# Later divisions in the first mixers' attention, an early table load, a moved turn of y, and x turned in three pieces at a residual add

## The chip, the cores and the metric

The program runs on one core of one Trainium2 chip. The metric is the device time of one execution in microseconds (us). The engines are TensorE (PE in the rows, with its weight loads as PEld), VectorE (DVE), ScalarE (ACT), GpSimd (POOL) and SyncE (SP), which issues nearly all transfers. Each engine works through its own list of instructions in order and waits on semaphores that the others raise.

## The reference, cut to what matters

Twelve sublayers work on a state x of 256 rows by 1024 columns: feed-forward, mixer, feed-forward, four times over. The first two blocks use the mixer below (called the first mixers here), the last two another one, which the change leaves as it was.

```python
for l in range(DEPTH):                                   # DEPTH = 2
    h = rms_norm(x, ffn1_norm[l])
    x = x + FFN_RES_WEIGHT * swiglu(h, ffn1_wg[l], ffn1_wu[l], ffn1_wd[l])
    h = rms_norm(x, mix_norm[l])
    z = h @ w_in[l]
    rq, rk, rv, rg, mq, mk, mv, ca, cg = jnp.split(z, cuts, axis=-1)
    y_ret  = silu(rg) * normed(retention(rotary(rq), rotary(rk), rv))   # 6 heads of 64
    y_moba = moba_attention(rotary(mq), rotary(mk), mv)                 # 6 heads of 64
    y_conv = conv_module(ca, cg, conv_w[l], conv_b[l], conv_ln_g[l], conv_ln_b[l])  # 31 taps
    x = x + concatenate([y_ret, y_moba, y_conv]) @ w_out[l]
    h = rms_norm(x, ffn2_norm[l])
    x = x + FFN_RES_WEIGHT * swiglu(h, ffn2_wg[l], ffn2_wu[l], ffn2_wd[l])
```

With 256 rows there is one block of keys, so `moba_attention` is a causal softmax over 256 keys: scores, a mask, exp, a division by the row's sum, and the product with the values.

## The kernel before, in words

All products run at near full float32 accuracy: weight and activation are each split into a high part (`wh`, `xh`, by ACT) and a low part (`wl`, `xl`, by DVE), and TensorE adds three products: L1759 high by high, L1760 low weight by high, L1762 high weight by low. A weight arrives in one of four `raw` buffers, is split by ACT at L2076 into one of five `wh` slots and by DVE at L2357 into the `wl` slot of the same number. A "sub" is two blocks of 128 rows of a weight: 12 matmuls. In a mixer the high parts are made four subs ahead of the one that TensorE takes, the low parts three ahead.

The order is written out once, in class `Order`; every engine's class runs through the same calls and issues only its own share. So the place of a call in `Order` sets its place in the lists of all engines at the same time.

**Turning x.** Activations must stand with their columns on the partitions before TensorE can use them. `turn_x` transposes x on TensorE (L1732, 128 by 128, out of the identity in `cst`), `prep_hi` (ACT, L2103) and `prep_lo` (DVE, L2404) split the result, scaled by the norm's gain. x has two tiles of rows, t = 0 and 1, and two halves of columns, h = 0 and 1; a sublayer's last output GEMM ends with the sub-products of (t 0, h 1) and then (t 1, h 1), each followed by the addition to x on DVE (L2442 in feed-forwards, L2444 in mixers). The five sublayers that are followed by a plain norm end in `leave`. Before the change h = 0 is turned whole (8 transposes) during the second half's GEMM, and `leave` turns h = 1: four transposes of t = 0, then four of t = 1, which wait for the last addition.

**Attention of the first mixers.** Six heads go in three groups of two (`attention`). For each group: scores on TensorE (L1878); on DVE the mask, with the row's extreme (L2472); exp on ACT with the row's sum (L2150); then `normalize`: two reciprocals on DVE (L2482) and four divisions on ACT (L2166, the exp's rows times the reciprocal). Then come the transposes of the group's probabilities (`turn`: L1732 reading `pt`, three into bank 6 for the first head, three into bank 7 for the second), their copies to `ptT` by ACT (L2156), and the product with the values (`values`: L1904, always into bank 7), whose result ACT and DVE split into `y1h` (L2171) and `y1l` (L2497). Bank 7 is free again only when `y1l` is done, or, after transposed heads, when ACT has copied them (`Trq`, L2180).

Between these stand calls of `fill`, which take one sub each of the projection GEMMs (mv, rq, rk, rv, rg) and, when a chunk is complete, what belongs to it. For rq and rk that is `q_done`: three taps of the convolution on both column blocks (DVE, six instructions, L2536), two copies of the chunk's rows to `zt` (ACT, L2188), and the rotation (DVE, six instructions, L2511 to L2516). Its transposed heads are posted to a later `fill` (L1732 reading `zt`, into banks 6 and 7). In the first mixers the function handed in is `step_fill`: a `fill` and one more tap per `fill` (two instructions) if no chunk was completed. The second and third group have two subs before the values of the group before (`half` 0), and two behind them.

**After the attention** comes the retention, pair by pair (`ret_values`: L1959 to L1961, always into bank 7), mixed with the output GEMM's first subs. `turn_wo` turns normalized rows of `ym` (L1732 reading `ym`) into bank 6 or 7 in turn, and ACT (L2176) and DVE (L2502) split them. The bank is free when DVE is done. `turn_wo(0)` writes bank 7, in both versions.

Of the kernel before, what the change touches and what calls it, by code (L numbers as in the profile page):

```python
# [394 lines left out]
class Order:  # L395
# [248 lines left out]
        pass  # L644

    def prep(self, h, nx):
        p = self.prep_turn(h, (self.next_t(), self.next_t()))
        self.prep_hi(p, nx)
        self.prep_lo(p, nx)

    def prep_turn(self, h, bb):
        out = []
        for n in range(2):
            out.append((4 * h + 2 * n, bb[n], self.new(self.s.turned, "x")))
        self.turn_x(h, out)
        return out

    def turn_x(self, h, p):
        pass

    def prep_hi(self, p, nx):
# [16 lines left out]

    def enter(self, nx):

        for n, p in enumerate(self.prep_turn(0, (6, 7)) + self.prep_turn(1, (2, 3))):
            self.prep_hi([p], nx)
            self.prep_lo([p], nx)
            self.ahead(min(n + 1, 3), 0)
        for h in range(2):
            for t in range(2):
                self.square(t, h)
        self.row_scale()

    def leave(self, nx, bb):  # L690
        p = self.prep_turn(1, bb)
        self.prep_hi(p, nx)
        self.prep_lo(p, nx)
        self.square(1, 1)
        self.row_scale()

# [130 lines left out]
    def into_x(self, label, banks2, X, K, ready, ga, nx, hook, start=None, td=None):  # L827
        plain, turned, p = nx[0] == "plain", False, None
        for h in range(2):
            b, k = start[h] if start else (banks2(), 0)  # L830
            end = K if h == 0 else max(k, K - (4 if plain else 2 * TAIL))
            while k < end:
                n, td = self.gemm_sub(label, b, X, k, K, ready)
                k += n
                hook(h, k)
                if h == 1 and k == 4 and plain:
                    self.prep(0, nx)
                    turned = True
            if h == 0:
                b0 = b  # L840
                if isinstance(ga, tuple):
                    self.need_ada(ga[0], 6)
                if start and not plain:
                    self.ahead(5, 0)
                for t in range(2):
                    self.add_x(t, h, b[t], td, ga)
                for t in range(2):
                    self.square(t, 0)
        if not plain and nx[-1] is not None:
            self.need_ada(nx[-1], 4)  # L850
        self.split_sums()
        self.flush()
        two = [self.take(label) for _ in range((K - k) // 2)]
        self.ahead(3 if plain else 2, 0)
        first, last = (self.s.prod, ("tail", two[0][0])), (self.s.sub, two[-1][0])
        self.x_sum = last
        self.tail(0, two, b[0], X, k, K, ready)
        if plain and not turned:
            p = self.prep_turn(0, (self.next_t(), self.next_t()))
        self.add_x(0, 1, b[0], first, ga)  # L860
        if p:
            self.prep_hi(p, nx)
        self.square(0, 1)
        self.tail(1, two, b[1], X, k, K, ready)
        if plain:
            self.add_x(1, 1, b[1], last, ga)
            if p:
                self.prep_lo(p, nx)
            self.leave(nx, b0)
            return  # L870
        self.normed(0, nx)

        def add_1(between=lambda: None):
            self.add_x(1, 1, b[1], last, ga, between)
        if nx[-1] is not None:
            self.half = nx, add_1
            return
        add_1()
        self.square(1, 1)
        self.normed(1, nx)  # L880
# [93 lines left out]
    def attention(self, groups, fill, last):  # L974

        n = len(groups)
        for g in range(n + 1):
            if g:
                self.turn(groups[g - 1])
            if g < n:  # L980
                self.scores(groups[g])
            else:
                last(0)
            ahead = [st for st in groups[g + 1] if st.pre is not None] if g + 1 < n else []
            for st in ahead:
                st.pre[0](st)
            subs = 1 if g == 0 else len(groups[min(g, n - 1)])
            for half in range(2 if g < n else 1):
                if half == 1 and len(ahead) == 2:
                    ahead[1].pre[1](ahead[1])  # L990
                for i in range(subs):
                    fill()
                    if i == 0 and half == 0:
                        if ahead:
                            ahead[0].pre[1](ahead[0])
                        if g < n:
                            self.normalize(groups[g])
                    if g == n:
                        last(i + 1)
                if g and half == 0 and groups[g - 1].pairs:  # L1000
                    self.values(groups[g - 1])
# [176 lines left out]
    def mix1(self, l, nx):  # L1178
# [57 lines left out]
            self.fill()  # L1236
            taps(1)

        def step_fill():
            n = len(self.jobs)  # L1240
            self.fill()
            taps(1 if len(self.jobs) == n else 0)

        steps = []
# [56 lines left out]
        def turn_wo(i):  # L1301
            tiles = (WO_TILES[1][1:],) + WO_TILES[2:]
            after = [[yret.get(0)], [normed], [yret.get(1), yret.get(2)]][i]
            pos = (3, 4, 6)[i]
            done = self.turn_y(tiles[i], after, pos, "y1")
            for n in range(len(tiles[i])):
                ytok[pos + n] = done
# [30 lines left out]
        ret_norm(0)  # L1338
        step()
        self.ret_sum(l, 1)  # L1340
        turn_wo(0)
        step()
        ret_out(2)
        ret_norm(1)
        step()
# [50 lines left out]
    def mix2(self, l, a, nx):  # L1396
# [197 lines left out]
            if i < 2:  # L1594
                gates(0, i)

        self.attention(groups, self.fill, last_values)
        while len(self.jobs) > 1 or self.jobs[0]["k"] < 6:
            self.fill()
        last_b = self.jobs[0]["b"]  # L1600
# [124 lines left out]
class Tensor(Order):  # L1725
# [59 lines left out]
        e.matmul(m.ps[b], m.onesr[:, :], m.ach[:, :], start=True, stop=False)  # L1785
        self.then_inc(e.matmul(m.ps[b], m.onesr[:, :], m.acl[:, :], start=False, stop=True), (s.prod, ("red", q)))

    def turn_x(self, h, p):
        m = self.m
        for t in range(2):  # L1790
            for k, b, tk in p:
                self.wait_ge(self.xr[t, h], self.free[b])
                for kk in range(2):
                    ins = self.transpose(m.ps[b][:, kk * 256 + t * P:kk * 256 + (t + 1) * P],
                                         m.x[:, t, (k + kk) * P:(k + kk + 1) * P])
                if t:
                    self.then_inc(ins, tk)
# [250 lines left out]
class Scalar(Order):  # L2048
# [144 lines left out]
    def glu(self, b, tk, u):  # L2193
        m = self.m
        for t in range(2):
            self.wait_ge(tk, self.rr_at, self.zt_free[0])
            self.then_inc(self.e.activation(m.zt[0][:, t, 0:256], m.ps[b[t]][:, 256:512], ACT.Sigmoid,
                                            scale=m.rr[:, t:t + 1]), (self.s.act, ("sigmoid", u[t][1])))

    def turn_u(self, b, after, tk, tp):  # L2200
        m = self.m
# [720 lines left out]
```

## Time and profile before

| | us |
|---|---|
| median of three runs | 2228.94 |
| lowest, highest | 2228.0, 2229.93 |
| the profiled execution, its own time | 2229.7 |
| its span in the trace | 2227.9 |
| PE busy, of the span | 2196.3 (99%) |
| DVE busy | 1536.2 (69%) |
| ACT busy | 1153.5 (52%) |
| POOL busy | 53.3 (2%) |

All times of rows are us from the span's start. The stages that the change touches are the first mixers, which lie at about 202 to 319 and 696 to 815, and the five ends of sublayers at 201, 318, 505, 695 and 814. A matmul is modelled as pipelined: a row's start against the next row's start is its share of time, its duration is longer. "x6" is six like instructions in one row. A bracket behind a row tells how long the engine stood idle before it and what ended that. Idle time of TensorE is time of the program unless it is made up later; idle time of the others costs nothing as such.

### The profile page before, as it was taken

What the parts mean: (1) busy time and instruction counts of PE and PEld (TensorE: products, weight loads), DVE (VectorE), ACT (ScalarE), POOL (GpSimd) and SP (SyncE); (2) the same over time, 40 slices, a digit from 0 to 9 for tenths busy, and PEclk for the clock granted to TensorE, in tenths of its full rate; (3) what the DMA queues carried; (4) which work ended last, traced back from release to release, by engine and by line L of the source; (5) the groups of instructions that cost most, each with busy time, mean ns of one, the idle gap of its engine ahead of it and who ended that gap; (6) DMA issues with size and microseconds to landing.
All of it is one profiled execution on the core that took longest, in us unless ns stands there. A gap on an engine that the chain in (4) does not pass through costs nothing.

```text
span 2227.9 us, 27041 instructions
## 1 busy us (share of the span) xinstructions
PE 2196.3 (99%) x10840; PEld 1842.4 (83%) x10840; DVE 1536.2 (69%) x2342; ACT 1153.5 (52%) x1782; POOL 53.3 (2%) x46
## 2 busy tenths in 40 slices
PE   8999999999999999999999999999999999999998
PEld 7888888888888888887888987888888889778887
DVE  5655975557886978867886655878678856557664
ACT  5445654444445654445445666544454456556443
POOL 0000010000000010001001000100000010001000
PEclk9999999999999999999999999999999999999999
DMA  8554454556875457775876444578768864445653
GB/s 287 191 194 155 150 177 171 188 195 232 284 280 161 150 192 264 264 263 180 282 277 193 157 133 148 187 269 284 265 215 283 286 192 140 144 151 171 235 198 123
DMA packets 250641, 462.92 MB, mean 208 GB/s; under 512 B 9798, under 2 KB 55792, under 8 KB 250388
## 3 DMA queue, kind: packets, MB, share of 16 engines
q1 hardware_dynamic: 250276, 461.04, 61.5%
q8 instruction: 85, 1.39, 0.2%
q14 instruction: 40, 0.33, 0.0%
q10 hardware_dynamic: 240, 0.16, 0.0%
HBM read 460.12 MB, written 1.05 MB: 207 GB/s over the span
## 4 chain that ended last, share of the span: by engine, by line
PE 91%; DVE 6%; ACT 2%; issue 0%; DMA 0%; POOL 0%; ACTq 0%; DVEq 0%; POOLq 0%
PE ps L1759 18%; PE ps L1762 18%; PE ps L1760 18%; PE s L1759 8%; PE s L1762 8%; PE s L1760 8%; PE ps L1732 4%; DVE wl L2357 1%; PE s L1878 1%; PE ps L1775 1%; PE ps L1773 1%; PE ps L1774 1%; PE ps L1904 1%; PE ps L1805 1%; DVE gts L2712 1%; PE ps L1838 1%
## 5 line engine op out<-in xcount | busy, mean ns | idle before, releaser
L2357 DVE TENSOR_TENSOR wl<-raw,wh 128x1024 fp32r<-128x1024 f32 (+2 forms) x732 | 851.1, 1180 | 219.0 <-ACT wh L2076 213.6
L2076 ACT ACTIVATE wh<-raw 128x1024 fp32r<-128x1024 f32 (+2 forms) x744 | 750.4, 1026 | 471.0 <-PE ps L1762 266.7
L1759 PE MATMUL ps<-wh,xh 128*128 128x512 f32 (+3 forms) x1632 | 621.5, 381 | 1.0 <-DVE wl L2357 1.0
L1762 PE MATMUL ps<-wh,xl 128*128 128x512 f32 (+3 forms) x1632 | 610.6, 374 | 0.0
L1760 PE MATMUL ps<-wl,xh 128*128 128x512 f32 (+3 forms) x1632 | 610.4, 374 | 0.0
L1759 PEld LDWEIGHTS ps<-wh,xh 128*128 128x128 f32 x1632 | 307.4, 188 | 55.7 <-issue 9.0
L1762 PEld LDWEIGHTS ps<-wh,xl 128*128 128x128 f32 x1632 | 307.2, 188 | 47.4
L1760 PEld LDWEIGHTS ps<-wl,xh 128*128 128x128 f32 x1632 | 307.7, 189 | 44.7
L2365 DVE SCALAR_TENSOR_TENSOR acc<-raw,condT,acc 128x512 f32<-128x512 f32 x252 | 188.7, 749 | 5.1
L1759 PE MATMUL s<-wh,xh 128*128 128x512 f32 x384 | 150.3, 391 | 0.0
L1762 PE MATMUL s<-wh,xl 128*128 128x512 f32 x384 | 149.6, 390 | 0.0
L1760 PE MATMUL s<-wl,xh 128*128 128x512 f32 x384 | 149.5, 389 | 0.0
L1759 PE MATMUL s<-wh,hTh 128*128 128x512 f32 x352 | 138.5, 393 | 0.0
L1762 PE MATMUL s<-wh,hTl 128*128 128x512 f32 x352 | 137.3, 390 | 0.0
L1760 PE MATMUL s<-wl,hTh 128*128 128x512 f32 x352 | 137.1, 390 | 0.0
L2143 ACT ACTIVATE hTh<-ps 128x512 fp32r<-128x512 f32 x88 | 48.3, 596 | 162.7 <-PE ps L1732 162.7
L2464 DVE TENSOR_TENSOR hTl<-ps,hTh 128x512 fp32r<-128x512 f32 x88 | 57.0, 686 | 104.3 <-ACT hTh L2143 104.3
L1759 PE MATMUL ps<-wh,hTh 128*128 128x512 f32 x268 | 104.5, 390 | 0.0
L1762 PE MATMUL ps<-wh,hTl 128*128 128x512 f32 x268 | 104.3, 389 | 0.0
L1760 PE MATMUL ps<-wl,hTh 128*128 128x512 f32 x268 | 104.3, 389 | 0.0
L1762 PEld LDWEIGHTS s<-wh,xl 128*128 128x128 f32 x384 | 72.1, 188 | 15.1
L1759 PEld LDWEIGHTS s<-wh,xh 128*128 128x128 f32 x384 | 72.1, 188 | 14.8
(348 smaller groups left out, 2495.0 us busy)
## 6 DMA issues: line engine op xcount, KB each, us to landing
raw<-in_ffn_w_in SPq DMA_DIRECT2D x80, 1024.0 KB, 5.3
raw<-in_ada_w SPq DMA_DIRECT2D x72, 1024.0 KB, 5.6
raw<-in_ffn_wg SPq DMA_DIRECT2D x40, 1024.0 KB, 5.3
raw<-in_ffn_wu SPq DMA_DIRECT2D x40, 1024.0 KB, 5.3
raw<-in_ffn_wd SPq DMA_DIRECT2D x40, 1024.0 KB, 5.2
raw<-in_ffn_w_out SPq DMA_DIRECT2D x40, 1024.0 KB, 5.7
raw<-in_mix_w_in SPq DMA_DIRECT2D x28, 1024.0 KB, 5.2
raw<-in_w_in SPq DMA_DIRECT2D x28, 768.0 KB, 4.5
```

What stands on the lines that cost most here:

```text
L1732: return self.e.transpose(out, src, self.m.ident[0:n, 0:n])
L1759: e.matmul(o, X[0](kk, t), hi, start=kk == 0, stop=False)
L1760: e.matmul(o, X[0](kk, t), lo, start=False, stop=False)
L1762: ins = e.matmul(o, X[1](kk, t), hi, start=False, stop=kk == K - 1)
L1773: e.matmul(o, X[0](kk, t), hi, start=kk == 0, stop=False)
L1774: e.matmul(o, X[0](kk, t), lo, start=False, stop=False)
L1775: ins = e.matmul(o, X[1](kk, t), hi, start=False, stop=kk == K - 1)
L2076: ins = self.e.activation(m.wh[j % NH][:, 0:n], m.raw[u % NR][:, k0 * w:k0 * w + n], ACT.Copy)
L2143: self.then_inc(self.e.activation(m.hTh[:, k:k + 2, :].rearrange("p k s -> p (k s)"), m.ps[b], ACT.Copy), th)
L2357: ins = self.e.tensor_tensor(m.wl[j % NH][:, 0:n], m.raw[u % NR][:, k0 * w:k0 * w + n], hi, ALU.subtract)
L2365: ins = self.e.scalar_tensor_tensor(out=a, in0=m.raw[u % NR][:, k * 512:k * 512 + 512], scalar=m.condT[:, kk:kk + 1], in1=a if kk else m.b ...
L2464: self.then_inc(self.e.tensor_tensor(lo, m.ps[b], hi.bitcast(F32), ALU.subtract), tl)
```

## The change

It does four things. First, in the first mixers `normalize` of a group is called inside the step: for the first group behind the `fill` but ahead of the step's tap; for the second and third group not in the first of the two steps but in the second one (`i == subs - 1`), behind everything that `fill` issues there. In the second mixers the order is as before. Second, behind the sigmoid of the convolution's gate ACT gets a one-element exp, so that the exp table is loaded there and not at the first softmax. Third, a `step` (one sub) that stood behind `turn_wo(0)` now stands ahead of it. Fourth, h = 0 of x is turned early in its first bank alone (4 transposes and not 8); `leave` turns (t 0, h 1), then the other bank of h = 0 (4 transposes, both tiles), then (t 1, h 1), and splits the three banks behind that.

```diff
--- before.py
+++ after.py
@@ -644,18 +644,20 @@
         pass
 
     def prep(self, h, nx):
-        p = self.prep_turn(h, (self.next_t(), self.next_t()))
+        p = self.prep_turn(h, {0: self.next_t()})
         self.prep_hi(p, nx)
         self.prep_lo(p, nx)
 
+    def prep_new(self, h, bb):
+
+        return [(4 * h + 2 * n, bb[n], self.new(self.s.turned, "x")) for n in bb]
+
     def prep_turn(self, h, bb):
-        out = []
-        for n in range(2):
-            out.append((4 * h + 2 * n, bb[n], self.new(self.s.turned, "x")))
-        self.turn_x(h, out)
-        return out
-
-    def turn_x(self, h, p):
+        p = self.prep_new(h, bb)
+        self.turn_x(h, p, range(2))
+        return p
+
+    def turn_x(self, h, p, rows):
         pass
 
     def prep_hi(self, p, nx):
@@ -678,7 +680,7 @@
 
     def enter(self, nx):
 
-        for n, p in enumerate(self.prep_turn(0, (6, 7)) + self.prep_turn(1, (2, 3))):
+        for n, p in enumerate(self.prep_turn(0, {0: 6, 1: 7}) + self.prep_turn(1, {0: 2, 1: 3})):
             self.prep_hi([p], nx)
             self.prep_lo([p], nx)
             self.ahead(min(n + 1, 3), 0)
@@ -688,9 +690,13 @@
         self.row_scale()
 
     def leave(self, nx, bb):
-        p = self.prep_turn(1, bb)
-        self.prep_hi(p, nx)
-        self.prep_lo(p, nx)
+
+        p0, p1 = self.prep_new(0, {1: self.next_t()}), self.prep_new(1, dict(enumerate(bb)))
+        self.turn_x(1, p1, (0,))
+        self.turn_x(0, p0, range(2))
+        self.turn_x(1, p1, (1,))
+        self.prep_hi(p0 + p1, nx)
+        self.prep_lo(p0 + p1, nx)
         self.square(1, 1)
         self.row_scale()
 
@@ -856,7 +862,7 @@
         self.x_sum = last
         self.tail(0, two, b[0], X, k, K, ready)
         if plain and not turned:
-            p = self.prep_turn(0, (self.next_t(), self.next_t()))
+            p = self.prep_turn(0, {0: self.next_t()})
         self.add_x(0, 1, b[0], first, ga)
         if p:
             self.prep_hi(p, nx)
@@ -989,12 +995,16 @@
                 if half == 1 and len(ahead) == 2:
                     ahead[1].pre[1](ahead[1])
                 for i in range(subs):
-                    fill()
-                    if i == 0 and half == 0:
-                        if ahead:
+
+                    norm = half == 0 and g < n and i == (subs - 1 if groups[g][0].by_act else 0)
+                    matrix = half == 0 and i == 0 and ahead
+
+                    def behind():
+                        if matrix:
                             ahead[0].pre[1](ahead[0])
-                        if g < n:
+                        if norm:
                             self.normalize(groups[g])
+                    fill(behind)
                     if g == n:
                         last(i + 1)
                 if g and half == 0 and groups[g - 1].pairs:
@@ -1236,9 +1246,10 @@
             self.fill()
             taps(1)
 
-        def step_fill():
+        def step_fill(norm):
             n = len(self.jobs)
             self.fill()
+            norm()
             taps(1 if len(self.jobs) == n else 0)
 
         steps = []
@@ -1338,8 +1349,8 @@
         ret_norm(0)
         step()
         self.ret_sum(l, 1)
+        step()
         turn_wo(0)
-        step()
         ret_out(2)
         ret_norm(1)
         step()
@@ -1594,7 +1605,11 @@
             if i < 2:
                 gates(0, i)
 
-        self.attention(groups, self.fill, last_values)
+        def fill(norm):
+            self.fill()
+            norm()
+
+        self.attention(groups, fill, last_values)
         while len(self.jobs) > 1 or self.jobs[0]["k"] < 6:
             self.fill()
         last_b = self.jobs[0]["b"]
@@ -1785,9 +1800,9 @@
         e.matmul(m.ps[b], m.onesr[:, :], m.ach[:, :], start=True, stop=False)
         self.then_inc(e.matmul(m.ps[b], m.onesr[:, :], m.acl[:, :], start=False, stop=True), (s.prod, ("red", q)))
 
-    def turn_x(self, h, p):
-        m = self.m
-        for t in range(2):
+    def turn_x(self, h, p, rows):
+        m = self.m
+        for t in rows:
             for k, b, tk in p:
                 self.wait_ge(self.xr[t, h], self.free[b])
                 for kk in range(2):
@@ -2196,6 +2211,8 @@
             self.wait_ge(tk, self.rr_at, self.zt_free[0])
             self.then_inc(self.e.activation(m.zt[0][:, t, 0:256], m.ps[b[t]][:, 256:512], ACT.Sigmoid,
                                             scale=m.rr[:, t:t + 1]), (self.s.act, ("sigmoid", u[t][1])))
+
+        self.e.activation(m.small[:, 240:241], m.phalf[:, 0:1], ACT.Exp)
 
     def turn_u(self, b, after, tk, tp):
         m = self.m
```

What stands in a row on the engines, at the three places that matter. Line numbers of the changed kernel are 15 to 17 higher for the same operation.

DVE, second group of a first mixer. Before; `RECIPROCAL` belongs to the second group's division, the six rows with `rt` and `zt` are the rotation of rq:

```order
L2357 TENSOR_TENSOR wl_64<-raw_53,wh_59 128x768
L2536 SCALAR_TENSOR_TENSOR cacc<-upad,cols_68,cacc 128x256 x2
L2482 RECIPROCAL small<-small 128x2 x2
L2357 TENSOR_TENSOR wl_65<-raw_54,wh_60 128x768
L2536 SCALAR_TENSOR_TENSOR cacc<-upad,cols_68,cacc 128x256 x6
L2511 TENSOR_TENSOR rt_131<-zt_104,cos_72 128x384
L2512 TENSOR_TENSOR rt_132<-zt_104,sin_73 128x384
L2513 TENSOR_TENSOR rt_133<-zt_104,cos_72 128x384
L2514 TENSOR_TENSOR rt_134<-zt_104,sin_73 128x384
L2515 TENSOR_TENSOR zt_104<-rt_131,rt_132 128x2x6x32
L2516 TENSOR_TENSOR zt_104<-rt_133,rt_134 128x2x6x32
L2497 TENSOR_TENSOR y1l<-ps,y1h 128x256
```

DVE at the same place in the changed kernel:

```order
L2553 SCALAR_TENSOR_TENSOR cacc<-upad,cols_68,cacc 128x256 x2
L2374 TENSOR_TENSOR wl_65<-raw_54,wh_60 128x768
L2553 SCALAR_TENSOR_TENSOR cacc<-upad,cols_68,cacc 128x256 x6
L2528 TENSOR_TENSOR rt_131<-zt_104,cos_72 128x384
L2529 TENSOR_TENSOR rt_132<-zt_104,sin_73 128x384
L2530 TENSOR_TENSOR rt_133<-zt_104,cos_72 128x384
L2531 TENSOR_TENSOR rt_134<-zt_104,sin_73 128x384
L2532 TENSOR_TENSOR zt_104<-rt_131,rt_132 128x2x6x32
L2533 TENSOR_TENSOR zt_104<-rt_133,rt_134 128x2x6x32
L2499 RECIPROCAL small<-small 128x2 x2
L2514 TENSOR_TENSOR y1l<-ps,y1h 128x256
```

The two reciprocals moved behind a `wl`, six tap instructions and the rotation, and stand directly ahead of `y1l`. The third group is the same, with rk.

ACT, second group. Before; `pt_107` and `pt_108` are the two heads' probabilities, divided in four instructions:

```order
L2076 ACTIVATE wh_60<-raw_54 128x768
L2166 ACTIVATE pt_107<-pt_107,small 128x128
L2166 ACTIVATE pt_107<-pt_107,small 128x256
L2166 ACTIVATE pt_108<-pt_108,small 128x128
L2166 ACTIVATE pt_108<-pt_108,small 128x256
L2076 ACTIVATE wh_61<-raw_54 128x768
L2188 ACTIVATE zt_104<-ps,rr 128x384 x2
L2171 ACTIVATE y1h<-ps 128x256
L2076 ACTIVATE wh_57<-raw_55 128x768
```

ACT at the same place in the changed kernel:

```order
L2091 ACTIVATE wh_60<-raw_54 128x768
L2091 ACTIVATE wh_61<-raw_54 128x768
L2203 ACTIVATE zt_104<-ps,rr 128x384 x2
L2181 ACTIVATE pt_107<-pt_107,small 128x128
L2181 ACTIVATE pt_107<-pt_107,small 128x256
L2181 ACTIVATE pt_108<-pt_108,small 128x128
L2181 ACTIVATE pt_108<-pt_108,small 128x256
L2186 ACTIVATE y1h<-ps 128x256
L2091 ACTIVATE wh_57<-raw_55 128x768
```

The divisions moved behind a `wh` and the two `zt`, and stand directly ahead of `y1h`. In the third group the transposed heads' copies `Trq` stand between the two `wh`, so the divisions moved behind them too.

PE around `turn_wo(0)`. Before (the two transposes of `ym`, then a whole sub of 12 matmuls, of which the first three rows are shown, then the retention's products, not shown):

```order
L1762 MATMUL ps<-wh_60,y1l 128x512
L1732 MATMUL ps<-cst,ym 128x128 x2
L1759 MATMUL ps<-wh_61,y1h 128x512
L1760 MATMUL ps<-wl_66,y1h 128x512
L1762 MATMUL ps<-wh_61,y1l 128x512
```

PE in the changed kernel:

```order
L1774 MATMUL ps<-wh_61,y1h 128x512
L1775 MATMUL ps<-wl_66,y1h 128x512
L1777 MATMUL ps<-wh_61,y1l 128x512
L1747 MATMUL ps<-cst,ym 128x128 x2
L1974 MATMUL ps<-rv,pt_107 128x64
L1975 MATMUL ps<-rv,pt_107 128x64
L1976 MATMUL ps<-rv,pt_107 128x64
```

The transposes of `ym` moved behind that sub, and the retention's products, which write the same bank 7, follow them directly.

## Rows read from the trace of the kernel before

**Rows 1.** What TensorE waited for in the whole program: us, times, longest:

```profile
PE ps L1904 <- ACT Trq L2180: 3.8, 2, 1.9
...
PE s L1732 <- DVE x L2442: 1.0, 3, 0.3
```

**Rows 2.** Timeline (start, duration, instruction), PE, a sublayer's end:

```profile
200.35 0.60 PE L1732 MATMUL s<-cst,x 128*128 128x128 f32 x4
201.30 0.66 PE L1732 MATMUL s<-cst,x 128*128 128x128 f32 x4 [0.35 <-DVE x L2442]
```

**Rows 3.** The same place, DVE:

```profile
200.55 0.69 DVE L2442 SCALAR_TENSOR_TENSOR x<-ps,x 128x512 f32<-128x512 f32 x1 [2.03 <-PE ps L1775]
```

**Rows 4.** Timeline, PE, attention of the first mixer without its subs:

```profile
256.74 0.91 PE L1732 MATMUL ps<-cst,pt 128*128 128x128 f32 x6
257.58 0.93 PE L1878 MATMUL s<-Tmk,Tmq 64*128 64x128 f32 x8
...
265.47 0.87 PE L1904 MATMUL ps<-ptT,mv 128*64 128x256 f32 x8 [1.92 <-ACT Trq L2180]
270.56 0.82 PE L1732 MATMUL ps<-cst,pt 128*128 128x128 f32 x6
271.13 0.42 PE L1759 MATMUL ps<-wh,xh 128*128 128x384 f32 x1
```

**Rows 5.** Timeline, DVE, first group's masks, then second and third group:

```profile
241.72 0.08 DVE L2472 DVE_READ_ACCUMULATOR2_ANT small<- 128x1 f32 x1
...
253.63 0.55 DVE L2511 TENSOR_TENSOR rt<-zt,cos 128x384 f32<-128x384 f32 x1
...
256.57 0.42 DVE L2497 TENSOR_TENSOR y1l<-ps,y1h 128x256 fp32r<-128x256 f32 x1
...
262.99 0.22 DVE L2482 RECIPROCAL small<-small 128x2 f32<-128x2 f32 x2
263.18 0.96 DVE L2357 TENSOR_TENSOR wl<-raw,wh 128x768 fp32r<-128x768 f32 x1
264.06 2.46 DVE L2536 SCALAR_TENSOR_TENSOR cacc<-upad,cols,cacc 128x256 f32<-128x256 f32 x6
```

**Rows 6.** Timeline, ACT, table load and the groups:

```profile
240.73 1.28 ACT L2150 ACT_TABLE_LOAD   x1
242.03 0.41 ACT L2150 ACTIVATE pt<-pt,small 128x128 f32<-128x128 f32 x1
...
260.54 0.40 ACT L2150 ACTIVATE pt<-pt,small 128x128 f32<-128x128 f32 x1 [2.37 <-DVE small L2472]
...
262.31 0.83 ACT L2076 ACTIVATE wh<-raw 128x768 fp32r<-128x768 f32 x1
263.18 1.49 ACT L2166 ACTIVATE pt<-pt,small 128x128 f32<-128x128 f32 x4
264.57 0.84 ACT L2180 ACTIVATE Trq<-ps 128x512 f32<-128x512 f32 x2
```

**Rows 7.** Timeline, PE, turn of ym:

```profile
294.59 0.44 PE L1732 MATMUL ps<-cst,ym 128*128 128x128 f32 x2 [0.24 <-DVE ym L2600]
...
297.62 0.33 PE L1959 MATMUL ps<-rv,pt 128*128 128x64 f32 x2
```

**Rows 8.** The same place, ACT:

```profile
295.06 0.38 ACT L2176 ACTIVATE y1h<-ps 128x256 fp32r<-128x256 f32 x1 [0.50 <-PE ps L1732]
```

**Rows 9.** Second mixer, PE, same places as rows 4:

```profile
759.58 1.42 PE L1904 MATMUL ps<-ptT,mv 128*64 128x256 f32 x8 [1.92 <-ACT Trq L2180]
...
766.25 0.81 PE L1732 MATMUL ps<-cst,pt 128*128 128x128 f32 x6
```

**Rows 10.** Stretches: us; busy (count) of PE, PEld, DVE, ACT, POOL; clock; DMA:

```profile
194.00:330.00 136.00, 132.90 (x751) 117.54 (x750) 107.73 (x225) 82.54 (x155) 6.91 (x6) 1.00 0.49 155
...
260.00:270.00 10.00, 8.08 (x52) 7.41 (x51) 9.36 (x27) 8.38 (x21) 0.00 (x0) 1.00 0.53 171
...
755.00:765.00 10.00, 8.08 (x43) 7.09 (x42) 9.35 (x24) 7.83 (x21) 0.00 (x0) 0.83 0.41 136
```

## Prediction

> **What bounds the kernel now.** I read the busy times first: TensorE is busy 99% of the span, so only what adds to or takes from its list or its idle time counts. Then the waits of TensorE [rows 1]: those at this change are two waits of 1.9 us for `Trq`, one in each first mixer, and short ones for the last addition to x, three of 0.35 in feed-forwards shown and two like them in mixers. Then the timelines around them, engine by engine. The reader is to see in [rows 4] that TensorE has its last sub before `values` behind it at 265.47 - 1.92 = 263.55, and in [rows 6] why it waits: ACT does the four divisions (263.18) ahead of the `Trq` copies (264.57), and these free bank 7. In [rows 5] DVE's y1l starts at 256.57, directly behind the rotation, and TensorE's `turn` starts at 256.74 [rows 4] and needs that y1l for its second bank: DVE sets that point with nearly no slack.
>
> **Part 1, x turned in three pieces: a gain.** The number of transposes stays 16 at each of five places; four move from an earlier point, where TensorE is never idle, into the wait. Four cost (201.30 - 200.35) less the wait. The first four start at 200.35, the next at 201.30, a distance of 0.95 [rows 2]; DVE's addition ends at 200.55 + 0.69 = 201.24 [rows 3]. At 0.11 each (0.57 over six in [rows 4], 270.56 to 271.13, gives 0.095) four take 0.38 to 0.44, so the distance holds eight of them and 0.1 is left. Gain 0.43 each, 2.15 over five. Behind it ACT splits three banks in a row and not two; the first product needs only the bank that was turned early, and the next one comes a sub later, so I count nothing. Bounds: 0.35 (the idle time shown) and 0.51 (the whole wait) each, 1.75 to 2.55.
>
> **Part 2, the table load.** It takes 1.28 and ends at 242.03, where the first exp starts [rows 6]. Without it exp starts when DVE has read out the row's extreme, at 241.72 + 0.08 = 241.80 [rows 5], and a signal, 241.85: 0.18 earlier. Everything that hangs on ACT there comes that much earlier. Bounds 0 and 0.23. In its new place it costs ACT 1.28 and an exp of at most 0.41. ACT is busy 82.5 of 136 us in this stretch [rows 10] and its `wh` run four subs ahead, which hides it; without that cover it would be 1.7 a mixer.
>
> **Part 3, the divisions of the second and third group: a loss.** The aim shows in the third group: `Trq` comes before the divisions. But `normalize` as a whole moved, reciprocals included, and DVE reaches them only behind six taps and the rotation. ACT blocks at the divisions until then, and queued behind them on ACT is `y1h`; behind that, on DVE, `y1l`; behind that, on TensorE, the second bank of `turn`. A chain that ran beside the rotation now runs after it.
>
> Second group, on the clock of the trace. The rotation ends at 256.57 [rows 5], less the 0.18 of part 2: 256.39. Reciprocal and its signal 0.2 (0.19 from 262.99 to 263.18): 256.6. Four divisions 1.4 (263.18 to 264.57 [rows 6]): 258.0. `y1h` 0.38 (size of [rows 8]) and signal: 258.41. `y1l` 0.42 [rows 5] and signal: 258.9, where before it was 257.05. So the second three transposes, and the scores behind them, are 1.85 late.
>
> Third group. DVE's list from y1l to the masks is the same and without idle time, so the exps, released at 260.54 before [rows 6], come at 262.4 and end 1.77 later, at 264.15. One `wh` (0.75 to 0.87) and now at once the `Trq` copies: 264.95. TensorE could start `values` 0.9 later (264.57 to 265.47): 265.85, against 265.47. The second group's loss eats the gain, and 0.4 is lost. DVE meanwhile: the second `wl` waits for its `wh`, 265.0; `wl` 0.88 and six taps 2.38 [rows 5] end at 268.3; the rotation takes 256.57 - 253.63 = 2.94, to 271.2 (its rows, two copies of `zt`, are there at 267.5). Then the same chain: reciprocal 271.4, divisions to 272.8, y1h to 273.2, y1l to 273.65, second bank of the turn at 273.7, three transposes 0.33: 274.0. Before, the sub there starts at 271.13 [rows 4]. Loss 2.9 in each first mixer, 5.8 together, as the two mixers' rows agree (265.47 and 759.58 with the same 1.92). Behind it nothing is owed: all weights' splits are at least a sub early, and retention starts when TensorE does. Bounds: 1.2 each, if the second bank waited for the divisions alone and not for y1l (y1h and y1l, 0.85 with signals, out of the chain in both groups), and 3.6, if the early table gives nothing and each of the chain's five links takes 0.1 more.
>
> **Part 4, `turn_wo(0)` a sub later: a small loss.** The wait that it is to remove is 0.4 (0.24 as idle time, the distance from the last matmul 0.4 more than usual) [rows 7]. But the transposes now write bank 7 directly ahead of the retention's products, which write bank 7 too. Without the wait the sub would start at 294.19 and end at 296.9; two transposes; ACT's y1h starts 0.47 behind their start (294.59 to 295.06, [rows 7, 8]), at 297.4, takes 0.38; y1l 0.42; signals 0.1: 298.3. Before, the products started at 297.62 [rows 7]. Loss 0.65 each, 1.3 together. Bounds: 0 (the split overlaps something that I don't see) and 1.9 a mixer (a `wl` of 1.2 ahead of y1l on DVE still running).
>
> **Sum.** 5.8 + 1.3 - 2.15 = +4.95. On the profiled execution (span 2227.9, its own time 2229.7) that is 2234.6; it lies 0.76 above the median of the runs, and the range of the runs, 1.9, is as wide as the clock item below. I set it on the median: 2228.94 + 4.95 = 2233.9.
>
> **The clock.** In the second mixer the 1.92 us wait is followed by a stretch at the lower level: the granted clock is 0.83 over 755 to 765, against 1.00 over 260 to 270 behind the same wait in the first [rows 10]. From `values` to `turn` it takes 766.25 - 759.58 = 6.67 [rows 9] against 270.56 - 265.47 = 5.09 [rows 4]: a fall to 1.2 GHz costs 1.58 here and follows one of two like waits. The changed kernel has no single wait of 1.92, but two near each other in the third group (about 0.9 and 1.4 with two or three transposes between) and two smaller in the second. A fall in the second group would be covered by the third group's wait. I count as many falls as before, one, and keep zero and two.
>
> The Trainium skill, in "TensorE: Matmul & The Clock Gate", section "Why this matters for your kernels", warns only of idle gaps that are clearly longer than all those here. By that rule the changed kernel would have no fall at all. The trace disagrees for a gap of 1.92, after which the clock did fall once.
>
> **Rivals.**
> A, no fall of the clock: no single new wait is as long as 1.92. The 1.58 goes: +3.4, 2232.3. For it: the waits are split. Against: together they are longer than before. Chance 0.25.
> B, falls in both first mixers: +6.5, 2235.5. For it: the pair of waits is 2.3 in 2.8 us. Chance 0.25.
> C, on the other side, faster: the divisions' new place doesn't decide, because DVE has done the rotation long before TensorE is at the `turn`. It would need the rotation to end 2.2 us earlier, before 254.4. Then `Trq` is copied at 263.2, `values` starts at 264.1, 1.4 earlier, and with the table 0.18: -3.2 for both, -2.15 for x, +1.3 for part 4, and with the clock -1.6: 2223.3 to 2224.9. Against: taps and rotation stand without a gap up to 256.57. Chance 0.07.
> D, the chains overlap more than I see, by the lower bounds of parts 3 and 4: 2.4 + 0 - 2.15: +0.25, 2229.2. Chance 0.08.
> My forecast as it stands: 0.35.
>
> **Range and chances.** 0.2% is 4.5 us, about what a measurement can tell from no change, and my sum lies just above it. Faster is C: 0.07. Within 0.2%: A and D whole, and a part of the forecast's own spread of about 1 us: 0.35. Slower: 0.58. The range goes from D's side, 2230.3, to above B, 2237.5; what is left out is C, most of D and the upper bounds.
>
> **What would show it.** Right: in the trace after, TensorE waits at `turn` for `y1l` in the second and third group, about 1.5 us each; ACT idle ahead of the divisions, released by the reciprocal; `values` waits well under 1 us; the retention's third products wait about 1 us for a y1l; no wait of 0.35 at the five additions. Wrong: if `turn` starts without a wait in the third group, part 3 falls and with it the sign; if x's five places still wait, part 1; if the falls of the clock are of another number, the time is off by 1.6 for each.

## The result, and the profile after

| | before | after |
|---|---|---|
| median, us (13 runs each) | 2228.52 | 2234.96 |
| lowest, highest | 2226.69, 2230.17 | 2232.63, 2236.64 |
| the profiled execution, its own time | 2229.7 | 2233.15 |
| its span | 2227.9 | 2231.3 |

The ratio is 1.0029, with a 95% interval of 1.0022 to 1.0037: 4.9 to 8.2 us slower. The forecast was 2233.9 in a range of 2230.3 to 2237.5, the forecast sum +4.95.

The waits of TensorE in the changed kernel (us in total, times, longest) show the signs that were named; only the waits for `y1l` at the turns, named as about 1.5 each, are 1.07. The two waits of 1.9 for `Trq` [rows 1] and the five for the addition to x are gone; new are four waits for `y1l` at the turns, and two at the retention's products. Of the waits for `Trq` one of 0.4 is left, in the first mixer:

```profile
PE ps L1747 <- DVE y1l L2514: 4.3, 4, 1.1
...
PE ps L1974 <- DVE y1l L2519: 1.9, 2, 0.9
...
PE ps L1747 <- ACT pt L2181: 1.4, 3, 0.8
...
PE ps L1919 <- ACT Trq L2195: 0.4, 1, 0.4
```

To lay one timeline on the other a common point is needed. The first transposes of `hb`, long before the change, stand here before:

```profile
46.62 1.03 PE L1732 MATMUL ps<-cst,hb 128*128 128x128 f32 x8
```

and here after:

```profile
44.67 1.03 PE L1747 MATMUL ps<-cst,hb 128*128 128x128 f32 x8
```

This execution was 1.95 us ahead before the change had touched anything: the loads at the program's start vary. The x turn at 200 adds 0.46, so 2.41 is added to a row of after in the first mixer to put it on the clock of the rows before.

TensorE after, second and third group of the first mixer, without the subs:

```profile
254.62 0.84 PE L1747 MATMUL ps<-cst,pt 128*128 128x128 f32 x3 [0.31 <-ACT pt L2181]
256.52 0.52 PE L1747 MATMUL ps<-cst,pt 128*128 128x128 f32 x3 [1.07 <-DVE y1l L2514]
256.97 0.93 PE L1893 MATMUL s<-Tmk,Tmq 64*128 64x128 f32 x8
...
263.34 0.87 PE L1919 MATMUL ps<-ptT,mv 128*64 128x256 f32 x8 [0.42 <-ACT Trq L2195]
...
269.41 0.83 PE L1747 MATMUL ps<-cst,pt 128*128 128x128 f32 x3 [0.81 <-ACT pt L2181]
271.32 0.52 PE L1747 MATMUL ps<-cst,pt 128*128 128x128 f32 x3 [1.07 <-DVE y1l L2514]
```

What was one row of six transposes [rows 4] is now two rows of three, each behind a wait. The scores stood at 257.58, now at 256.97 + 2.41 = 259.38: 1.80 late. `values` stood at 265.47, now at 265.75: 0.28 late, although its wait shrank from 1.92 to 0.42. DVE after, the same two groups:

```profile
253.50 0.55 DVE L2533 TENSOR_TENSOR zt<-rt,rt 128x384 f32<-128x384 f32 x1
253.97 0.22 DVE L2499 RECIPROCAL small<-small 128x2 f32<-128x2 f32 x2
255.95 0.42 DVE L2514 TENSOR_TENSOR y1l<-ps,y1h 128x256 fp32r<-128x256 f32 x1 [1.76 <-ACT y1h L2186]
...
268.76 0.22 DVE L2499 RECIPROCAL small<-small 128x2 f32<-128x2 f32 x2
270.75 0.43 DVE L2514 TENSOR_TENSOR y1l<-ps,y1h 128x256 fp32r<-128x256 f32 x1 [1.76 <-ACT y1h L2186]
```

and ACT after:

```profile
254.16 1.49 ACT L2181 ACTIVATE pt<-pt,small 128x128 f32<-128x128 f32 x4 [3.93 <-DVE small L2499]
255.56 0.36 ACT L2186 ACTIVATE y1h<-ps 128x256 fp32r<-128x256 f32 x1
...
268.96 1.49 ACT L2181 ACTIVATE pt<-pt,small 128x128 f32<-128x128 f32 x4 [3.99 <-DVE small L2499]
```

Read the three together. ACT stands idle for 3.93 us, released by the reciprocal, which DVE starts only as the rotation ends. Then DVE is idle for 1.76, released by `y1h`, and TensorE for 1.07, released by `y1l`. The idle times pass from engine to engine, which is the mark of a chain made serial.

### The profile page after: what moved, and what is told of

Same layout as the page of the kernel before. It is cut to its first block, busy times and chain, and to the rows that moved or that the text cites. A ratio compares the mean times of both kernels' runs of the same rounds, so it can differ in the third digit from the quotient of the medians.

```text
span 2231.3 us, 27045 instructions
## 1 busy us (share of the span) xinstructions
PE 2197.6 (98%) x10840; PEld 1842.8 (83%) x10840; DVE 1537.0 (69%) x2342; ACT 1153.7 (52%) x1784; POOL 55.2 (2%) x46
## 4 chain that ended last, share of the span: by engine, by line
PE 90%; DVE 7%; ACT 2%; DMA 0%; issue 0%; POOL 0%; ACTq 0%; DVEq 0%; POOLq 0%; SPq 0%
PE ps L1774 18%; PE ps L1777 18%; PE ps L1775 18%; PE s L1777 8%; PE s L1774 7%; PE s L1775 7%; PE ps L1747 3%; DVE wl L2374 2%; DVE cacc L2553 1%; PE s L1893 1%; PE ps L1790 1%; PE ps L1788 1%; PE ps L1789 1%; PE ps L1919 1%; PE ps L1820 1%; DVE gts L2729 1%
## 5 line engine op out<-in xcount | busy, mean ns | idle before, releaser
L2111 ACT ACTIVATE junk<-x 128x512 f32<-128x512 f32 x56 | 35.6, 636 | 95.0 <-DVE x L2461 59.1
```

Of the source, the lines that this page charges most:

```text
L2111: self.then_inc(self.e.activation(m.junk[:, :], m.x[:, t, h * 512:(h + 1) * 512], ACT.Square, scale=1.0 / 32, accum_out=m.ssq[:, 2 * h + t ...
```

## The experiments

Those with an interval were run side by side with the kernel before, whose median was 2228.8 beside x, turn_wo, the attention's part and the first of the two faster kernels, 2229.09 beside the single groups, the early reciprocals alone and the last of the faster kernels, and 2228.7 beside the table. "Faster" and "slower" in us are that median times the distance of the ratio from 1; the plain difference of the medians can differ from it by up to 0.8. "Landmark" means the start of a given row of TensorE, compared between two traces.

**One part alone: x.** Only the fourth edit of the change (`prep_turn` with one bank, `leave` with three pieces).

> The kernel before with x turned in three pieces at the five residual adds, and nothing else. Theory (the losses lie in the attention and at turn_wo(0), x is a gain): 2.2 us faster than before, 0.43 at each of the five places, and no wait of 0.35 left there. Rival (three banks split in a row cost what the filled wait gives): no change, and in the trace a new wait at the first products behind the turns.

Measured: 2226.61, ratio 0.9988 (0.9979 to 0.9996), 2.2 faster. The landmarks behind the five places come 0.43 to 0.46 earlier each, and all five waits are gone. Part 1 stands, with its size.

**One part alone: turn_wo(0).**

```diff
-        turn_wo(0)
         step()
+        turn_wo(0)
```

> The kernel before with turn_wo(0) moved behind the step, and nothing else. Theory: 1.3 us slower than before; the retention's third products wait about 0.95 us in each first mixer for y1l, which frees bank 7, and the wait of 0.4 at the transposes is gone. Rival (the move does what it seems to be for): 0.8 us faster, 0.4 at each of two places.

Measured: 2228.47, ratio 0.9998 (0.9989 to 1.0006). The time can't tell: 0.8 faster and 1.3 slower both lie within this interval. Nor can the two spans, as this profile lacks a fall of the clock in the second mixer that costs 1.6 in the one of before. TensorE's list can. The first retention products after the turn (297.62 before, [rows 7]):

```profile
297.95 0.43 PE L1959 MATMUL ps<-rv,pt 128*128 128x64 f32 x2 [0.93 <-DVE y1l L2502]
```

This trace runs 0.28 ahead at the third group's product with the values (276.99 before), so the row is 0.33 + 0.28 = 0.61 late, and as much in the second mixer. The wait of 0.24 for `ym` became one of 0.93 for `y1l`.

**One part alone: attention.** The new place of `normalize`, with x, table and turn_wo as before.

```diff
+    norm = half == 0 and g < n and i == (subs - 1 if groups[g][0].by_act else 0)
...
-                        if g < n:
+                        if norm:
                             self.normalize(groups[g])
```

> The kernel before with normalize called inside the step (reciprocals and divisions late in the second and third group), and nothing else. Theory: 6 us slower than before, less up to 1.6 where a fall of the clock behind the old wait of 1.9 us is gone; TensorE waits at turn for y1l in both groups. Rival (the loss comes from the early table load or the moved turn): no change or faster by up to 2.8, the two waits for Trq.

Measured: 2235.7, ratio 1.003 (1.002 to 1.004), 6.7 slower. The landmarks of the first mixer move by +3.06, those of the second by the same once the fall of the clock that before had there is taken out (+3.07 against the second profile of before, told below, which has none there). That is 6.1 for both mixers, beside 1.2 lost at turn_wo(0) and 2.2 gained at x: this part makes nearly all of the loss.

**Which group?** The same, for one group alone; for the third, `g == 2`:

```diff
-    norm = half == 0 and g < n and i == (subs - 1 if groups[g][0].by_act else 0)
+    norm = half == 0 and g < n and i == (1 if g == 1 and groups[g][0].by_act else 0)
```

> Only the second group's reciprocals and divisions go behind the last sub (the third group's stay in their old place; x, table and turn_wo as before). Theory (the chain reciprocal, divisions, y1h, y1l behind the rotation): the second three transposes of the turn at 257 us and the scores start 2.0 us late (1.85 and the 0.18 that the early table does not give here), the exps and the third group's divisions and Trq copies with them; `values` still waits about 1.9 for Trq, nothing is given back: +2.0 in each first mixer, 4.1 together, less up to 1.6 if the fall of the clock does not come. No wait for y1l at the third group's turn. Rival 1 (the loss arises in the third group alone; in the second, slack on ACT takes it up): the landmarks of TensorE at `values` move by less than 0.5, the time by less than 1. Rival 2 (the whole 3.1 of a mixer arises in the second group): +6.

> Only the third group's reciprocals and divisions go behind its last sub. Theory: the Trq copies come directly behind a wh, `values` starts 1.4 to 1.5 earlier in each first mixer and waits about 0.4; the rotation ends at about 269.4, reciprocals, four divisions, y1h and y1l follow, the second three transposes of the turn can start at 271.9 and the sub at 272.2, where it was 271.13: +1.1 a mixer, 2.2 together, within 1.6 for the clock. With the kernel of the second group alone this adds up to the 3.1 a mixer of both groups. Rival (the second group is innocent, all 3.1 come from the third): +6. Rival 2 (the aim is reached once the second group is left alone): the turn does not wait, 1.4 faster a mixer.

Measured: second group 2231.91, ratio 1.0015 (1.0006 to 1.0024), 3.3 slower; third group 2232.0, ratio 1.0011 (1.0002 to 1.002), 2.4 slower; together 5.7, beside 6.7 for both at once, within the intervals. (By the plain medians the two are 2.8 and 2.9, so the times don't rank them; the traces do.) TensorE with the second group alone late:

```profile
259.47 0.52 PE L1740 MATMUL ps<-cst,pt 128*128 128x128 f32 x3 [1.07 <-DVE y1l L2505]
259.91 0.93 PE L1886 MATMUL s<-Tmk,Tmq 64*128 64x128 f32 x8
...
267.67 0.87 PE L1912 MATMUL ps<-ptT,mv 128*64 128x256 f32 x8 [1.80 <-ACT Trq L2188]
```

and with the third alone late:

```profile
264.02 0.87 PE L1912 MATMUL ps<-ptT,mv 128*64 128x256 f32 x8 [0.39 <-ACT Trq L2188]
...
270.09 0.83 PE L1740 MATMUL ps<-cst,pt 128*128 128x128 f32 x3 [0.83 <-ACT pt L2174]
272.00 0.52 PE L1740 MATMUL ps<-cst,pt 128*128 128x128 f32 x3 [1.07 <-DVE y1l L2505]
```

The first of them is 0.35 behind before the attention begins. The scores are 1.98 late and `values` is 1.85 late, still behind a wait of 1.80 where it was 1.92: only 0.13 is given back. In the second, `values` comes 1.41 early, and the stretch from there through the turn with its two waits is 2.59 longer, +1.18 in all. Each group has its own loss, so both rivals that gave it one place fall, and 1.85 + 1.18 = 3.03 is the 3.06 of both. The second group's loss is what keeps the early `Trq` from paying.

**The reciprocals or the divisions?** Here the reciprocals go out in the step's first sub, ahead of its tap, and the divisions alone go behind the last sub.

```diff
                     def behind():
                         if matrix:
                             ahead[0].pre[1](ahead[0])
+                        if half == 0 and i == 0 and g < n:
+                            self.invert(groups[g])      # DVE: the reciprocals alone
                         if norm:
                             self.normalize(groups[g])   # ACT: the divisions alone
```

> Reciprocals go out in the step's first sub, ahead of the tap; the divisions behind the last one; x, table and turn_wo as before. Theory: no turn waits for the divisions; `values` starts 1.5 earlier in each first mixer, of which 0.7 to 0.75 is given back at the third group's turn, where y1l stands behind the rotation: 1.5 faster together, 3.1 if the fall of the clock after `values` goes as well. Rival (it was the divisions' place itself that cost, not the reciprocals'): 2 to 6 slower, the turns wait about 1 for y1l in both groups.

> The changed kernel with turn_wo(0) back in its old place, and with normalize in two parts: the reciprocals in the first step, ahead of the tap, in all three groups; the divisions on ACT in the last step. Theory (what costs is that the reciprocals moved behind the rotation on DVE, not that the divisions moved on ACT): turn no longer waits for y1l in the second and third group, Trq is copied 1.4 us earlier, values waits 0.5 and not 1.9: 2.2 for x, 0.4 for the table, 2.8 for the two waits, up to 1.6 for a fall of the clock: 5.4 to 7 us faster than before, about 2222. Rival (the divisions' place on ACT, behind two more wh and zt, delays y1h and with it bank 7 whatever DVE does): turn still waits over 1 us in each group, and the kernel is at most 1 us faster than before.

Measured: alone 2227.16, ratio 0.9991 (0.9982 to 0.9999), 2.0 faster; with x in three pieces and the early table (the changed kernel but for the reciprocals and turn_wo) 2224.65, ratio 0.998 (0.9971 to 0.9989), 4.5 faster. So the late place of the divisions costs nothing that shows; what made the loss is that DVE reached the reciprocals behind a `wl`, six taps and a rotation. The sum that I expected for the second, 5.4 to 7, was too good: it counted 2.8 for the two waits, and what follows shows that only about half of that was kept. TensorE in it, third group's turn:

```profile
266.82 0.49 PE L1756 MATMUL ps<-cst,pt 128*128 128x128 f32 x3
267.84 0.52 PE L1756 MATMUL ps<-cst,pt 128*128 128x128 f32 x3 [0.54 <-ACT ptT L2180]
```

DVE at the same place:

```profile
266.81 0.55 DVE L2545 TENSOR_TENSOR zt<-rt,rt 128x384 f32<-128x384 f32 x1
267.28 0.42 DVE L2526 TENSOR_TENSOR y1l<-ps,y1h 128x256 fp32r<-128x256 f32 x1
```

From the first group's scores on, TensorE now comes 1.6 earlier to the turn, 0.2 of it from the table, and 0.73 is given back there. The row names ACT's `ptT`, but `y1l`, done at 267.70, is a candidate too.

**Which of the two?** One tap of three is moved from ahead of the last rotation to a sub behind the turn, in the kernel just told.

```diff
             def done(b, tk):
-                taps(3)
+                taps(2 if n == "rk" else 3)
...
         def first_pair(i):
+            if i == 1:
+                taps(1)
```

> As the kernel with split reciprocals, x in three pieces and the early table, and one tap of three (two instructions of 0.41) moved from ahead of the last rotation to a sub behind the turn. What the trace of that kernel leaves open is what its third group's turn waits for (0.54, put down to ACT's ptT; DVE's y1l ends 0.13 earlier). Theory 1 (y1l, which stands behind taps and rotation on DVE): y1l ends 0.8 earlier, the wait of about 0.6 at the second three transposes goes, 0.6 to 0.75 gained in each first mixer: 5.5 to 6 faster than the kernel before. Theory 2 (ACT's ptT behind two wh): the wait stays at 0.5 and the time at 4.5 faster than before.

Measured, in five runs: 2222.45, ratio 0.9967 (0.9955 to 0.998), 7.4 faster than before (4.5 to 10.0), the lowest median of all. Its interval overlaps that of the kernel just told; the traces tell the two apart: from the first group's scores to the third group's product with the values it takes 0.73 less in the first mixer and 0.77 less in the second. The turn is one row of six again:

```profile
266.89 0.82 PE L1758 MATMUL ps<-cst,pt 128*128 128x128 f32 x6
```

because on DVE

```profile
266.58 0.42 DVE L2528 TENSOR_TENSOR y1l<-ps,y1h 128x256 fp32r<-128x256 f32 x1
```

ends, at 267.00, before the second bank is wanted, while ACT starts `ptT` no earlier than in the other kernel (267.42, 267.34 there). So it was `y1l`, and the releaser in brackets was the wrong one; there `y1l` and `ptT` had ended 0.13 apart.

**The table alone.**

```diff
+        self.e.activation(m.small[:, 240:241], m.phalf[:, 0:1], ACT.Exp)
```

> Only the exp table is loaded early. Theory: the first exp of the first mixers starts 0.18 earlier and all behind it as far as the wait for Trq, where the same 0.18 stays gained: 0.36 faster together, not to be told from no change by the time; `values` starts at 265.3 from the same start, with the same wait of 1.9. Rival (the load in its new place delays a wh or the exps of another group): 0.5 to 3 slower.

Measured: 2229.0, ratio 1.0 (0.9991 to 1.0009). The first exp is 0.19 earlier, as forecast, but TensorE's turn of that group gains only 0.04 and `values` 0.02 (265.47 to 263.68, in a trace that is 1.77 ahead). DVE with the table alone:

```profile
242.51 0.23 DVE L2484 RECIPROCAL small<-small 128x2 f32<-128x2 f32 x2
```

and ACT:

```profile
242.71 1.50 ACT L2166 ACTIVATE pt<-pt,small 128x128 f32<-128x128 f32 x4
```

The first group's divisions wait for a reciprocal that stands behind a tap. In the changed kernel the reciprocal is ahead of that tap, at 241.09:

```profile
241.09 0.41 DVE L2499 RECIPROCAL small<-small 128x2 f32<-128x2 f32 x2
```

and there the first group's turn does gain 0.19. With the attention's part alone it gains 0.00. At this turn neither edit is worth more than 0.04 without the other.

**The same two kernels once more.** Both were profiled a second time, unchanged, for the clock.

> The kernel before, word for word, profiled once more. If the falls of the clock belong to a kernel's order of work, the granted clock is 0.83 over 755 to 765 and 1.00 over 1000 to 1010 as in the first trace. If they differ from execution to execution, the fall behind the wait for Trq at 759.6 may be absent (the times then 1.6 shorter from there on), while every wait and distance in TensorE's list is the same within 0.1.

> The changed kernel, word for word, profiled once more. By order of work: falls again at 754 (granted clock 0.83 over 750 to 760) and two between 1000 and 1020 (0.83 over 1000 to 1010, 0.84 over 1010 to 1020). By execution: at least one of the three is elsewhere or absent; the waits for y1l at the turns stay at four of about 1.07.

The second profile of before, stretches of the first and the second mixer behind their waits for `Trq` (columns as in rows 10):

```profile
260.00:270.00 10.00, 8.07 (x44) 7.03 (x43) 9.36 (x28) 7.60 (x20) 0.00 (x0) 0.83 0.60 180
...
755.00:765.00 10.00, 8.08 (x52) 7.41 (x52) 9.39 (x27) 7.52 (x20) 0.00 (x0) 1.00 0.60 185
```

In the first profile it was the other way round [rows 10]. So the place of the fall belongs to the execution and not to the kernel's list. After, first and then second profile:

```profile
750.00:760.00 10.00, 8.55 (x45) 7.18 (x45) 8.13 (x23) 7.67 (x21) 0.00 (x0) 0.83 0.35 107
```

```profile
765.00:775.00 10.00, 8.03 (x40) 7.21 (x39) 8.20 (x18) 5.14 (x11) 0.00 (x0) 0.83 0.30 91
```

Up to 814 these two second profiles have one fall each that costs time, so they can be laid over each other as the forecast did. Before, from the first transposes of `hb` to the last addition's first transposes in the second mixer:

```profile
47.23 1.03 PE L1732 MATMUL ps<-cst,hb 128*128 128x128 f32 x8
...
813.55 0.60 PE L1732 MATMUL ps<-cst,x 128*128 128x128 f32 x4
```

and after:

```profile
46.90 1.03 PE L1747 MATMUL ps<-cst,hb 128*128 128x128 f32 x8
...
818.11 1.60 PE L1747 MATMUL ps<-cst,x 128*128 128x128 f32 x12
```

766.32 and 771.21: 4.89 longer, where the sum said 4.95. All five gains at x lie in it: the fifth is four transposes that left their place ahead of the last row.

## Why the prediction was right

**Part 1.** Forecast 0.43 at each of five places, measured 0.43 to 0.46. The alone kernel is 2.2 faster, forecast 2.15.

**Part 2.** The first exp came 0.18 to 0.19 earlier, and in the changed kernel the turn of the first group too. That the table alone would bring it was my working, and that was wrong: the step "everything that hangs on ACT there comes that much earlier" left out that the divisions also hang on the reciprocal, behind a tap. It came out right by luck, because part 3 moves that reciprocal. For the sum, which took both, this changed nothing.

**Part 3.** The chain came out link by link. On the clock of before: reciprocal done at 253.97 + 0.22 + 2.41 = 256.60 (forecast 256.6), y1h started at 257.97 (divisions done, 258.0), second half of the turn at 258.93 (258.9), scores 1.80 late (1.85). `values` at 265.75 (265.85). Third group: second half of the turn at 271.32 + 2.41 = 273.73 (273.7). All of it 2.88 a mixer, forecast 2.9; the attention's part alone, without the early table, 3.06. The aim was reached, `Trq` did come early, and two things ate it, as forecast: the second group's loss and the third group's own chain. DVE also stands idle for 1.76 in each chain, with `wl` and taps queued behind `y1l`, which the text did not price. Nothing of it showed on TensorE.

The waits at the turns were named as about 1.5 each. They are two waits, 0.31 and 1.07 in the second group, 0.81 and 1.07 in the third: the first three transposes wait for the divisions already, which the text did not say.

**Part 4.** Forecast 0.65, measured 0.61 a mixer alone and 0.63 in the changed kernel (the wait for `y1l` is 0.93, the one that went 0.24).

**The sum.** +4.95 forecast, 4.89 by the traces with equal falls up to 814, +6.4 by the medians with an interval of 4.9 to 8.2, so the sum lies at the interval's lower end. (The median of before fell by 0.42 with ten more runs, so the forecast time itself is 1.1 below the measured one.) Behind 814 there is more, which I did not forecast. At the next blocks' conditioning sums TensorE waits for `acl`, in the first profile of after:

```profile
936.00 0.50 PE L1800 MATMUL ps<-ach,onesr 128*128 128x512 f32 x1 [0.26 <-DVE acl L2389]
```

which costs 0.43 there, 0.52 in the second profile, 0.42 with the attention's part alone, 0.19 with x alone and 0.82 in the fastest kernel, and nothing before or with turn_wo, the table or one late group alone. DVE reaches `acl` behind a `wl` that waits for ACT's `wh`. Why that `wh` is late was not settled. At the norm between 1004 and 1020, where the clock falls once or twice in every trace, the first pair of profiles differs by another 1.3 and the second by 0.2. The number of falls goes with it: from the first product with `dg` to the next conditioning sum the four traces with two falls there (the first of after, the attention's part alone, the third group alone, the early reciprocals alone) take 38.37 to 38.70, the nine with one 37.05 to 37.46. These two places can hold what lies between 4.9 and 6.4, but the runs do not show how much of it they hold in the median.

**The clock.** "As many falls as before, one" in the first mixers is what both pairs of profiles show, and that it came out so was luck, for the reason given was poor. I tied the fall to the long wait. In five traces with both waits of 1.9 (before twice, x, turn_wo and table alone) a fall followed in three of ten. In the changed kernel one came in the second group and one behind the third, so neither rival A (no fall) nor rival B (falls in both mixers) showed up in two profiles. With falls that vary like this, both may hold for some of the runs. That a fall in the second group is covered by the third group's waits was right. In the first profile of after, from the second group's scores to the transposed heads behind the third turn, in the first mixer without a fall and in the second with one:

```profile
256.97 0.93 PE L1893 MATMUL s<-Tmk,Tmq 64*128 64x128 f32 x8
...
273.77 0.82 PE L1747 MATMUL ps<-cst,zt 128*128 128x128 f32 x6
...
753.35 1.05 PE L1893 MATMUL s<-Tmk,Tmq 64*128 64x128 f32 x8
...
770.13 0.82 PE L1747 MATMUL ps<-cst,zt 128*128 128x128 f32 x6
```

16.80 and 16.78. In the second profile the fall came behind that cover: the third group's last wait ends at 769.92, and the stretches around it (columns as in rows 10) are

```profile
767.00:770.00 3.00, 1.03 (x6) 0.45 (x5) 1.24 (x5) 2.44 (x7) 0.00 (x0) 1.00 0.00 0
771.00:774.00 3.00, 3.00 (x12) 2.90 (x11) 3.00 (x7) 1.27 (x3) 0.00 (x0) 0.50 0.58 149
```

There the same distance, scores to transposed heads, is 18.20.

**Rival C**, faster, needed the rotation to end before 254.4 on the clock of before; it ends at 254.05 + 2.41 = 256.46. The kernel with early reciprocals alone shows what it is worth to be free of the rotation: 2.0 faster. **Rival D**, overlap unseen, fell with the 1.07 at each `y1l`.

The Trainium skill, "TensorE: Matmul & The Clock Gate", section "Why this matters for your kernels", names as the cause of such a fall only idle gaps longer than any wait in these mixers; by that line alone no fall would have come here. The falls at 750 to 760 and 765 to 775 in the changed kernel, whose waits there are 1.07 at most, speak against it more plainly than the one of before.

## What to carry to other kernels

When a step is moved, ask on every engine what it is queued behind in its new place. The divisions on ACT could move and gain; the reciprocals on DVE, which went along because one function issues both, landed behind a `wl`, six taps and the rotation and made a parallel chain serial. And a gain is often held by a second input: the early table and the early reciprocal gave 0.04 and 0.00 alone and 0.19 together, and the early `Trq` gave its second half only when a tap was out of the way of `y1l`.

## What the runs showed of the hardware

A fall of TensorE's clock from 2.4 to 1.2 GHz is not a fixed property of a list of instructions: the same kernel had it in the second mixer in one execution and in the first in another, at 1.6 us each time, and a fall in the changed kernel cost nothing where waits behind it took it up (16.78 us with and 16.80 without it). Inside a fall the granted clock is 0.50. A comparison of two profiles has to pair the falls before it speaks of 1 or 2 us.

A table load took 1.28 us wherever it stood. In its old place the next instruction started 0.02 behind it [rows 6], with no further cost to be seen; loaded early, it let the first exp start 0.19 earlier.
